# A two-block transformer kernel on one core: how the first block's attention outputs are split into a high and a low part

## The reference

```python
h = rms_norm(x, norm_mix[l])
z = h @ w_in[l]
q_a, k_a, v_a, q_b, k_b, v_b, g_a, g_b = jnp.split(z, offsets, axis=-1)
y_a = windowed_gqa(q_a, k_a, v_a, sink[l])        # softmax(q k + bias) v, 8 heads
y_b = neighborhood_attn(q_b, k_b, v_b, rpb[l])    # softmax(q k + bias) v, 8 heads
gates = sigmoid(concat([g_a, g_b]) + b_gate[l])
merged = gates[..., :D] * (y_a @ w_proj_a[l]) + gates[..., D:] * (y_b @ w_proj_b[l])
x = x + merged @ w_out[l]
h2 = rms_norm(x, norm_mlp[l])
x = x + square(relu(h2 @ w_up[l])) @ w_down[l]
```

## Time and profile before

| | us |
|---|---|
| device time, median of 3 runs | 1459.44 (1456.83 to 1459.45) |
| the profiled execution's span, first to last instruction | 1458.0 |
| TensorE matmul busy in it | 1441.4 (99%) |
| VectorE busy | 796.7 (55%) |
| ScalarE busy | 620.5 (43%) |
| GpSimd busy | 367.5 (25%) |
| share of TensorE in the chain that ended last | 93% |

### The profile page before, as it was taken

How to read it: one execution, slowest core, us unless ns; L and a number is a source line. 1 busy time by engine, 2 the same in 40 slices (tenths; PEclk the granted TensorE clock), 3 DMA queues, 4 the chain that set the end, 5 groups by cost and what they waited for, 6 DMA issues and landing times.

```text
span 1458.0 us, 18785 instructions
## 1 busy us (share of the span) xinstructions
PE 1441.4 (99%) x7061; PEld 1205.4 (83%) x7061; DVE 796.7 (55%) x1323; ACT 620.5 (43%) x971; POOL 367.5 (25%) x368
## 2 busy tenths in 40 slices
PE   9999999999999999999999999999999999999998
PEld 7888888888888888888888888888888888888886
DVE  5648864434443434334478795443447879543344
ACT  5436862234322323234434695333333469532332
POOL 3004521012000000000407785221120778510012
PEclk9999999999999999999999999999999999999999
DMA  5564333323322322322241123223224112323321
GB/s 195 85 126 119 104 109 93 109 87 106 107 87 87 116 87 89 112 86 88 71 137 47 30 63 109 87 87 116 87 76 134 51 33 55 109 87 104 99 88 58
DMA packets 160496, 135.64 MB, mean 93 GB/s; under 512 B 35928, under 2 KB 153952, under 8 KB 160416
## 3 DMA queue, kind: packets, MB, share of 16 engines
q1 hardware_dynamic: 160256, 134.50, 31.0%
q10 hardware_dynamic: 160, 0.07, 0.0%
HBM read 124.26 MB, written 2.92 MB: 87 GB/s over the span
## 4 chain that ended last, share of the span: by engine, by line
PE 93%; DVE 4%; ACT 1%; POOL 1%; issue 1%; DVEq 0%; ACTq 0%; POOLq 0%
PE G L1942 75%; PE G L1924 3%; PE S L1924 3%; PE T L2033 3%; PE G L2057 2%; PE G L2064 2%; PE G L2154 1%; DVE sq L1533 1%; POOL t L853 1%; PE G L2330 1%; PE G L2108 1%; PE G L1990 1%; ACT w L1053 1%; POOL z L949 0%; PE G L2160 0%
## 5 line engine op out<-in xcount | busy, mean ns | idle before, releaser
L1942 PE MATMUL G<-gx,w 128*128 128x512 f32 x2928 | 671.9, 390 | 1.3 <-DVE w L1396 1.3
L1942 PEld LDWEIGHTS G<-gx,w 128*128 128x128 f32 x2928 | 549.0, 188 | 116.7 <-DVE w L1396 1.7
L1396 DVE TENSOR_TENSOR w<-raw,w 128x2048 fp32r<-128x2048 f32 (+3 forms) x110 | 249.9, 2272 | 222.7 <-ACT w L1053 222.5
L1053 ACT ACTIVATE w<-raw 128x2048 fp32r<-128x2048 f32 (+2 forms) x112 | 207.8, 1855 | 126.4 <-PE G L1942 109.6
L1942 PE MATMUL G<-kvb,w 128*128 128x512 f32 x960 | 218.4, 389 | 0.0
L1942 PEld LDWEIGHTS G<-kvb,w 128*128 128x128 f32 x960 | 180.2, 188 | 37.4
L853 POOL TENSOR_TENSOR t<-t,rden 128x512 f32<-128x512 f32 (+2 forms) x128 | 108.8, 852 | 113.5 <-DVE rden L1539 111.4
L895 POOL TENSOR_TENSOR t<-sig 128x512 f32<-128x512 f32 x24 | 35.3, 1472 | 335.4 <-DVE sig L1607 335.4
L1670 DVE TENSOR_TENSOR x<-G,x 128x512 f32<-128x512 f32 x56 | 38.6, 688 | 115.3 <-PE G L1942 115.3
L993 POOL TENSOR_TENSOR sumsq_f<-sumsq_f,sq_f 128x512 f32<-128x512 f32 x7 | 9.1, 1295 | 333.5 <-ACT sq_f L1083 333.5
L1942 PE MATMUL G<-m,w 128*128 128x512 f32 x384 | 87.4, 389 | 0.0
(11 more groups left out here) (254 smaller groups left out, 1786.9 us busy)
## 6 DMA issues: line engine op xcount, KB each, us to landing
raw<-in_w_in SPq DMA_DIRECT2D x98, 512.0 KB, 7.1
raw<-in_w_up SPq DMA_DIRECT2D x32, 512.0 KB
raw<-in_w_down SPq DMA_DIRECT2D x32, 512.0 KB
raw<-in_w_out SPq DMA_DIRECT2D x24, 512.0 KB
raw<-in_w_attn_proj SPq DMA_DIRECT2D x8, 512.0 KB
raw<-in_w_fourier_proj SPq DMA_DIRECT2D x8, 512.0 KB
biasb<-bias_rows SPq DMA_DIRECT2D x24, 128.0 KB
xin<-in_x SPq DMA_DIRECT2D x4, 512.0 KB, 6.3
```

What stands on the lines that cost most here:

```text
L1053: nc.scalar.activation(high, cut(K.raw[:, j % 2, 0:n]), ACT.Copy).then_inc(K.w_hi, 1)
L1396: nc.vector.tensor_tensor(low, cut(K.raw[:, s, 0:n]), high.bitcast(F32), ALU.subtract).then_inc(K.w_lo, 1)
L1942: mm = nc.tensor.matmul(b[:, :], w(p, k), x(q, k), start=(k == i == 0), stop=(k == kts - 1 and i == len(PASSES) - 1))
```

## The change

The low part of block 1's attention outputs no longer comes from VectorE. ScalarE reads a head's bank twice: once as it is into a new fp32 tile `head_f` (128 x 512, one for all heads, even heads in its lower and odd heads in its upper half), once for the high part as before. GpSimd then subtracts, for two heads in one instruction of 128 partitions, the high part from `head_f`. It does so inside its loop `probabilities`, behind the multiply of iteration n at which the odd head's output is taken (n = 10, 18, ... 58), and for the last pair behind the loop. A bank is free for TensorE when ScalarE has taken the high part (`y_hi`). A semaphore `y_lo` counts the GpSimd steps: ScalarE waits for it before it overwrites `head_f` in the next even head, TensorE before the projections. The tile numbers G_ shift, since 16 counts of `tile_out` are gone.

```diff
@@ program_pool, probabilities
+            if A.kind != "L" and A.last_of(n) is not None and A.last_of(n) % 2 == 1:
+                out_low(A, A.last_of(n))
...
+        if A.kind != "L":
+            out_low(A, A.total // TT - 1)
+
+    def out_low(A, h):
+
+        t = h % HEADS // 2
+        q = K.qa if A.at(h * TT) == "A" else K.qb
+        pool.wait_ge(K.y_hi, h + 1)
+        nc.gpsimd.tensor_tensor(A.rows(h, q[:, 1, t, :]), A.in_order(h, K.head_f[:, :]),
+                                A.rows(h, q[:, 0, t, :]).bitcast(F32), ALU.subtract).then_inc(K.y_lo, 1)
@@ program_act, out_hi
+            if h >= 2 and e == 0:
+                act.wait_ge(K.y_lo, h // 2)
+            nc.scalar.activation(K.head_f[r, :], A.out_bank(h)[r, :], ACT.Copy).then_inc(K.y_all, 1)
             nc.scalar.activation(A.rows(h, q[r, 0, t, :]), A.in_order(h, A.out_bank(h)[r, :]),
                                  ACT.Copy).then_inc(K.y_hi, 1)
@@ program_vector, attention
-        def out(h):
...
-            nc.vector.tensor_tensor(A.rows(h, q[r, 1, t, :]), A.in_order(h, A.out_bank(h)[r, :]),
-                                    A.rows(h, q[r, 0, t, :]).bitcast(F32), ALU.subtract).then_inc(K.tile_out, 1)
...
-            if A.kind != "L" and A.last_of(n) is not None:
-                out(A.last_of(n))
...
-            out(total // TT - 1)
@@ program_pe, values
+            elif m % 2 == 0 and h < 2:
+                pe.wait_ge(K.tile_out, G_A - 1 + h)
             elif m % 2 == 0:
-                pe.wait_ge(K.tile_out, A.g_out(h).value() - 1)
+                pe.wait_ge(K.y_hi, h - 1)
@@ program_pe, merge and heads_ready
+                if g.k == G_MERGE:
+                    pe.wait_ge(K.y_hi, 2 * HEADS - 1 + m)
...
-        pe.wait_ge(K.tile_out, G_B + HEADS)
+        pe.wait_ge(K.y_lo, HEADS)
```

More of the change, by code:

```diff
@@ L77 @@
 J_END = J_L + LAYERS * JL
-G_X, G_IN, G_A, G_B, G_MERGE, G_OUT, G_MLP = 0, 8, 26, 34, 42, 74, 82
-G_L, GL = 146, 108
+G_X, G_IN, G_A, G_B, G_MERGE, G_OUT, G_MLP = 0, 8, 26, 26, 26, 58, 66
+G_L, GL = 130, 108
 F_X, F_IN, F_MERGE, F_OUT, F_MLP = 0, 8, 26, 58, 66
@@ L267, in allocate @@
     K.biasb = at("biasb", 77, [P, 2, 3, KH * WINDOW], F32)
+    K.head_f = at("head_f", 72, [P, SEQ], F32)
     K.sig1 = at("sig1", 74, [P, 4, SEQ], F32)
@@ L378, in allocate @@
     K.y_hi = semaphore("y_hi")
+    K.y_all = semaphore("y_all")
+    K.y_lo = semaphore("y_lo")
     K.z_in = [semaphore(f"z_in{i}") for i in range(2)]
```

## The result

| | before | changed |
|---|---|---|
| device time, median | 1459.4 us (4 runs, 1456.8 to 1459.5) | 1480.8 us (4 runs, 1479.3 to 1484.8) |
| ratio | | 1.0156, 95% interval 1.0143 to 1.0169 |
| span of the profiled execution | 1458.0 us | 1477.5 us |
| TensorE's first values matmul to the gate product | 121.61 to 203.19: 81.6 us | 118.72 to 223.02: 104.3 us |

The changed kernel is 21.4 us slower. 1483.4 was forecast, 1467 to 1491 as the range. All of it lies in the stage of the change.

The account below looks back on a forecast made before the run. Short loops between engines, not busy time, were taken to bound the stage. 14.5 (GpSimd's place) + 3.5 + 0.3 (ScalarE's copy) + 5.7 (clock) = 24.0 us on 1459.4 gave 1483.4 us, range 1467 to 1491.

Parts of the forecast that it names:

- ScalarE's second copy: Plain copy ahead of the exponentials: 0.5 us at each of seven even heads, 3.5 us, plus 0.3 at head 14.
- the low end of 0.1 each: Lower bound at even heads: the reciprocal of n + 2 starts about 0.1 us later; 0.7 us in all.
- GpSimd's place: Subtraction queued ahead of the multiply of n + 1 stalls TensorE at seven odd heads, 2.54 or 2.87 us; net 14.5.
- the waits that should vanish: TensorE's usual waits after each stall, 0.27 us each: three in A, two in B, taken off the stall.
- The clock: TensorE's clock falls to 0.50 behind half of the seven stalls, 1.6 us each: 5.7 us, ends 0 and 11.4.
- GpSimd's step is hidden: Rival: GpSimd's idle 1.97 us covers the step; 1464.3 us, up to 1472 with stalls half as long; chance 0.12.
- VectorE's relief wins: Rival: without VectorE's subtractions all TensorE waits for GpSimd could go, at most 7.5 us: 1452 us; chance 0.03.
- Reversed order slow on GpSimd: Rival: GpSimd's reversed reads in B take 2.8 us; heads 9, 11, 13 stall 1.45 longer: 1487.8 us; chance 0.09.

Follow-up runs that it names:

- the relief alone: Changed kernel without ScalarE's plain copy, GpSimd's step late and reading another tile, low parts left out: 1457.7 us (0.9989), stage 80.7.
- the kernel without the copy: Changed kernel without ScalarE's plain copy; GpSimd's step stays in place but reads another tile, low parts left out: 1475.1 us (1.0108).
- the doubled step: Changed kernel with GpSimd's subtraction made twice, the first time into sumsq: 1494.1 us (1.0242).

## Why the prediction was right

**What bounds the stage.** Right: short loops and not busy time. VectorE's busy time fell by 8.2 us (796.7 to 788.5) and the stage grew by 22.7; the relief alone is worth 0.9 to 1.6 us.

**ScalarE's second copy.** At even heads 0.5 was taken each, 3.5 in all; 0.42 to 0.50 came, 3.2. The step behind it, that a link which already waits passes a delay on in full, held; the low end of 0.1 each did not occur. At odd heads I took 0.62 from one copy's start to the next; it is 0.50 (129.10 to 129.59). The 0.62 in the earlier trace rows is the distance to the exponentials.

**GpSimd's place.** The steps came in the order that the sum has. The terms: GpSimd starts 1.15 behind the first copy (1.27 forecast), the subtraction takes 1.26 (1.35, from bounds of 1.295 and 1.395, both too long), TensorE follows at 3.04 (3.37). The delay of the transposes is 2.21 in A and 2.54 in B where the forecast has 2.54 and 2.87. In its parts the delay was 0.33 too long. Against this stand the waits that should vanish: I took 0.81 off in A and 0.54 in B; the distances say 2.21 - 1.67 = 0.54 in A and, with 1.56 taken off for a fall, 2.54 - 2.46, about 0.1, in B. The two errors are of nearly the same size and cancel: net 1.67 and 2.46 against 1.73 and 2.33. So this term, 14.5 us, is right in sum (5.0 in A, 7.4 and about 2.2 in B) partly by luck. The step that failed is that waits of weight loads count in full: in B it took 4.45 us from the transposes of n + 1 to the next output copy before (4.95 - 0.50) and 4.44 now (9.04 - 1.56 - 3.04). In the kernel without the copy, where no fall has to be taken off behind the stall of head 11, it took 4.46 (193.46 to 197.92). So the two waits there, of 0.25 and 0.16 us, had cost TensorE nothing. In the kernel before, the matmuls ahead of the first of them ran until 176.32, past the 176.13 at which the weights could be loaded:

```profile
175.69 0.63 PE L2108 MATMUL G<-gx,w 128*128 128x512 f32 x2
...
176.13 0.20 PEld L2033 LDWEIGHTS T<-ident,t 128*128 128x128 f32 x2 [0.25 <-POOL t L853]
...
177.00 0.26 PEld L2033 LDWEIGHTS T<-ident,t 128*128 128x128 f32 x2 [0.16 <-POOL t L853]
```

**The clock.** Half of the stalls were to be followed by a fall of 1.6 us. The profile has three of seven, a fall is worth 1.56 by the kernel without the copy. 4.7 us against 5.7. The price of a fall was read rightly; that half of the stalls would have one was a guess from a single case, and that it came near is luck. Other executions had more falls, by their mean clock: the slowest of the four, 1484.8 us, has a mean clock of 0.991 where the profiled one has 0.996. At half clock for the missing share, that is 2 x 0.005 x 1480 = 15 us more at the lower level, some four falls; its time is 5.4 us longer, which fits 4 x 1.56 = 6.2.

**The sum.** 24.0 forecast; 22.7 in the stage, 21.4 by the medians.

**The rivals.** (1) *GpSimd's step is hidden* did not happen in the place that the change gives it, but did once the step was moved: 1463.9 us, where that rival's sum has 1464.3. Its terms were less good, 3.2 for the even and 2.1 for the odd heads against 3.5 and 1.1. (2) *VectorE's relief wins*: only with both steps in idle places, and then by 1 to 2 us and not by 7.5. (3) *Reversed order slow on GpSimd*: no. The subtraction takes the same time in A and in B; by tile, with ns minimum, median and maximum:

```profile
L885 POOL TENSOR_TENSOR qa<-head_f,qa x4: 1265/1265/1267, 130.3 to 169.1; 128x512 fp32r<-128x512 f32 x4
L885 POOL TENSOR_TENSOR qb<-head_f,qb x4: 1258/1259/1296, 183.2 to 223.3; 128x512 fp32r<-128x512 f32 x4
```

The Trainium skill's "GPSIMD Engine Reference", section 7, has reads slow down only when the inner step is above 8 bytes. It does not speak of steps backwards; for one fp32 element backwards the trace shows no slowing either. The 1.11 us estimated from section 3.1 of that page was 0.15 too short, my 1.35 was 0.09 too long.

## What to carry to other kernels

On an engine that works its stream in order, an added instruction costs by what is queued behind it. Its length counts in full only once the slack ahead of that is used up: 1.3 us for seven steps by themselves, 1.24 for each step that lengthened a stall. So look at which instruction behind it is ready already and who waits for that one, and put the new step just ahead of the engine's own idle time. An idle share, or an idle gap in the timeline, is cover only for work whose inputs are there when the gap opens. Before taking work off a busy engine, take it away altogether in an experiment: here that showed 1 to 2 us to be had, and moving the two output steps by one head won more (2.6 us) than giving one of them to another engine (1.2 to 1.8 where its place cost nothing).

## What the runs showed of the hardware

The clock falls at waits that seem short. Waits of 1.9 to 2.6 us, with TensorE full before and after, were followed by a fall to the lower level (0.50) for about 3.4 us in six of fourteen cases (the changed kernel and the one without the copy), all six in B, where the waits are 2.1 and 2.6 us; waits of 1.65 to 1.88 in none of seven; waits of 3.6 to 3.8 in six of seven. Which of the stalls in B is spared changes from kernel to kernel (head 13, head 11, and head 9 with the doubled step); what decides it, the runs leave open.

That it is not the length alone shows at the start of the kernel too. There every one of the fourteen profiles has the same wait of 1.88 us. In the profile of before it was followed by a fall, and 12 matmuls then took 4.58 us; in that of the changed kernel by none, and they took 3.01:

```profile
8.36 3.01 PE L2166 MATMUL G<-gx,w 128*128 128x512 f32 x12 [1.88 <-DVE w L1421]
```

Nine of the fourteen profiles have this fall. In them TensorE goes on at 8.94 to 9.65 us of the span, in the five without it at 8.25 to 8.44; no run shows why.

In the two profiles here, the fall and a start 1.3 us earlier make the 2.9 us before the stage, by which the two spans differ less than the stages do. The fall at the start costs 1.57 us, as much as one in the stage, so the number of falls is a large part of what one kernel's executions differ by.
